# A two-block transformer kernel in fp32: the second feed-forward product accumulated over 16 k-tiles at a time instead of 8, and the adaLN loads of one gate moved ahead of the recurrence

## What is computed

```
mod = silu(c) @ w_ada + b_ada                 # 2048 x 12288, six groups g = 0..5
shift1, scale1, gate1, shift2, scale2, gate2 = split(mod, 6)
...                                           # block 1: pooling and stick-breaking attention
x = x + gate1 * (mixed @ w_o)                 # block 2: dilated attention and a gated recurrence
h2 = rms_norm(x, norm2_w) * (1 + scale2) + shift2
f = square(relu(h2 @ w_ff1)) @ w_ff2          # 2048 x 8192, then 8192 x 2048
x = x + gate2 * f
```

## Time and profile before

| | |
|---|---|
| median of three runs | 2578.6 us |
| the profiled execution | 2580.78 us |
| its span, first to last instruction | 2579.0 us |
| PE busy | 2512.8 us, 97% |
| DVE busy | 2021.8 us, 78% |
| ACT busy | 1276.7 us, 50% |
| mean granted TensorE clock | 0.998 |
| read from HBM | 659.4 MB, 256 GB/s over the span |

### The profile page before, as it was taken

One profiled execution on the slowest core, in us unless ns is written; L12 is line 12 of the kernel. 1 busy time (PEld: TensorE's weight loads), 2 busy tenths in 40 slices (PEclk: granted clock), 3 DMA queues, 4 the chain that ended last, 5 costly groups with the idle time before them and its releaser, 6 DMA issues.

```text
span 2579.0 us, 32612 instructions
## 1 busy us (share of the span) xinstructions
PE 2512.8 (97%) x12429; PEld 2110.6 (82%) x12429; DVE 2021.8 (78%) x2305; ACT 1276.7 (50%) x1657; POOL 265.5 (10%) x321
## 2 busy tenths in 40 slices
PE   6999999999999999999999999999999999999998
PEld 5878787877888888888887878887888888888887
DVE  6778979998988898989877798886865666665566
ACT  4544455334555445544445554556455544554453
POOL 1000120202020202020300001350000000020000
PEclk9999999999999999999999999999999999999999
DMA  9999869897989898989756766464566777766654
GB/s 347 332 346 328 300 194 354 321 337 243 325 292 350 286 367 279 355 292 357 267 169 224 234 198 185 141 225 164 189 215 227 231 225 230 233 213 189 194 189 147
DMA packets 298364, 663.66 MB, mean 257 GB/s; under 512 B 20752, under 2 KB 21104, under 8 KB 297184
## 3 DMA queue, kind: packets, MB, share of 16 engines
q1 hardware_dynamic: 294976, 650.21, 74.4%
q0 software_dynamic: 2656, 9.66, 1.1%
q10 hardware_dynamic: 576, 1.70, 0.2%
HBM read 659.39 MB, written 2.10 MB: 256 GB/s over the span
## 4 chain that ended last, share of the span: by engine, by line
PE 83%; DVE 8%; DMA 3%; issue 3%; ACT 3%; SPq 0%; DVEq 0%; POOL 0%; ACTq 0%
PE PS L645 82%; DVE WL L1520 3%; ACT WH L1107 2%; DVE ACC L1528 2%; DMA RAWX<-in_w_in 1%; DVE UQ L1520 1%; PE PS L648 1%; DMA RAW<-in_w_in 0%; DMA RAW<-in_w_ada 0%; DMA RAWX<-in_w_o 0%; DVE hn L1528 0%; DVE AL L1520 0%; DMA RAW<-in_w_ff 0%; DMA RAW<-in_w_a_up 0%; DMA RAW<-in_w_o 0%
## 5 line engine op out<-in xcount | busy, mean ns | idle before, releaser
L1107 ACT ACTIVATE WH<-RAW 128x1024 fp32r<-128x1024 f32 x569 | 602.5, 1059 | 770.2 <-PE PS L645 578.1
L1520 DVE TENSOR_TENSOR WL<-RAW,WH 128x1024 fp32r<-128x1024 f32 x569 | 710.9, 1251 | 341.3 <-ACT WH L1107 340.1
L645 PE MATMUL PS<-WH,AH 128*128 128x512 f32 x2052 | 811.5, 395 | 16.6 <-DVE WL L1520 9.8
L645 PE MATMUL PS<-WH,AL 128*128 128x512 f32 x2052 | 800.8, 390 | 0.0
L645 PE MATMUL PS<-WL,AH 128*128 128x512 f32 x2052 | 800.5, 390 | 0.0
L645 PE MATMUL PS<-HL,WH 128*128 128x512 f32 x2048 | 601.9, 395 | 6.3 <-DVE HL L1528 5.1
L645 PEld LDWEIGHTS PS<-WH,AH 128*128 128x128 f32 x2052 | 386.1, 188 | 103.4 <-DVE WL L1520 18.7
L645 PEld LDWEIGHTS PS<-WH,AL 128*128 128x128 f32 x2052 | 386.0, 188 | 81.9
L645 PEld LDWEIGHTS PS<-WL,AH 128*128 128x128 f32 x2052 | 386.3, 188 | 76.8 <-issue 0.2
L645 PEld LDWEIGHTS PS<-HL,WL 128*128 128x128 f32 x2048 | 349.4, 188 | 67.2
L645 PE MATMUL PS<-HL,WL 128*128 128x256 f32 x2048 | 364.0, 279 | 0.0
(11 more groups left out here) (251 smaller groups left out, 1966.2 us busy)
## 6 DMA issues: line engine op xcount, KB each, us to landing
RAW<-in_w_ff SPq DMA_DIRECT2D x337, 512.0 KB, 4.4
RAW<-in_w_ada SPq DMA_DIRECT2D x282, 512.0 KB, 5.1
RAW<-in_w_in SPq DMA_DIRECT2D x192, 512.0 KB, 4.5
RAWX<-in_w_ada SPq DMA_DIRECT2D x102, 512.0 KB, 5.6
RAWY<-in_w_ff SPq DMA_DIRECT2D x96, 512.0 KB, 4.1
RAWX<-in_w_ff SPq DMA_DIRECT2D x79, 512.0 KB, 5.5
RAWX<-in_w_in SPq DMA_DIRECT2D x48, 512.0 KB, 5.4
RAW<-in_w_out SPq DMA_DIRECT2D x32, 512.0 KB, 3.6
```

Of the source, the lines that this page charges most:

```text
L645: return e.matmul(o, l, r, start=start, stop=stop, skip_group_check=True)
L1107: return e.activation(o, i, f, **kw)
L1520: return e.tensor_tensor(o, a, b, op)
```

## The change

`ff2` now takes all 16 k-tiles of `AH`/`AL` at a time: four rounds of 32 `ff1` ticks and then four `ff2` blocks of 8 ticks, with no `ff1` block ahead. In `chunk_t` the second feed-forward part now also runs its pieces in pairs. In the load plan, the groups of the first feed-forward part are spread over weights 0 to 245 instead of 0 to 221 and are followed there by the first 16 items of group (1,2). The other 16 are spread over weights 6 to 29 of `in2` (ticks 454 to 477), where before 6 were spread over 4 to 27, 18 over 30 to 65 and 8 over 96 to 115.

```diff
     def ff(w1, w2):
         one = [w(w1, 0, 16, cb * 512) for cb in range(16)]
-        two = [[c for n in range(4) for c in w(w2, r * 8, 8, n * 512)] for r in range(8)]
-        out = one[0] + one[1]
-        for r in range(8):
-            if r < 7:
-                out += one[2 * r + 2] + one[2 * r + 3]
-            out += two[r]
-        return out
+        two = [[c for n in range(4) for c in w(w2, r * 16, 16, n * 512)] for r in range(4)]
+        return [c for r in range(4) for part in one[4 * r:4 * r + 4] + [two[r]] for c in part]
...
-    plan += spread(ff(I["w_ff1"][0], I["w_ff2"][0]), [ada1[5], ada2[0], ada2[1], ada2[3], ada2[4]], 0, 222, 10)
-    in2 = spread(in2, [ada2[2][24:]], 96, 116)
-    in2 = spread(in2, [ada2[2][6:24]], 30, 66)
-    plan += spread(in2, [ada2[2][:6]], 4, 28)
+    plan += spread(ff(I["w_ff1"][0], I["w_ff2"][0]), [ada1[5], ada2[0], ada2[1], ada2[3], ada2[4], ada2[2][:16]], 0, 246, 10)
+    plan += spread(in2, [ada2[2][16:]], 6, 30)
...
     def ff(name, at):
-        made = [(name + "1", cb, at + 8 * cb, 8) for cb in range(2)]
-        at += 16
-        for r in range(8):
-            if r < 7:
-                made += [(name + "1", 2 * r + 2 + c, at + 8 * c, 8) for c in range(2)]
-                at += 16
-            made += [(name + "2", 4 * r + n, at + 4 * n, 4) for n in range(4)]
-            at += 16
+        made = []
+        for r in range(4):
+            made += [(name + "1", 4 * r + c, at + 8 * c, 8) for c in range(4)]
+            made += [(name + "2", 4 * r + n, at + 32 + 8 * n, 8) for n in range(4)]
+            at += 64
         return made
...
-                b = 2 * (n % 4) if n < 28 else 2 * (n % 2)
+                b = 2 * (n % 4) if n < 12 else 2 * (n % 2)
...
-                    for run in ((0, 1), (2, 3)) if j < FG else ((0, 1, 2, 3),):
+                    for run in ((0, 1), (2, 3)):
...
-                    r = n // 4
-                    if n % 4 == 0 and c % 2 == 0:
-                        e.wait_ge(s_fl, (0 if name == "ff2" else 32) + 4 * r + 2 * (c // 2) + 2)
-                    if n == 31 and c == 3:
-                        chunk_end(j, q, c, AH, AL, 8 * (r % 2))
+                    if n % 4 == 0:
+                        e.wait_ge(s_fl, (0 if name == "ff2" else 32) + 2 * n + c + 1)
+                    if n == 15 and c == 7:
+                        chunk_end(j, q, c, AH, AL, 0)
                     else:
-                        chunk(j, q, c, c == 3, AH, AL, 8 * (r % 2))
+                        chunk(j, q, c, c == 7, AH, AL, 0)
...
-                k = 8 * (n // 2 % 2) + 4 * (n % 2) + 2 * t
+                k = 4 * (n % 4) + 2 * t
...
-                for name, at, step in (("wo", WO + 8, 8), ("ff2", IN2 - 12, 4), ("ob", OB + 4, 4)):
+                for name, at, step in (("wo", WO + 8, 8), ("ff2", IN2 - 24, 8), ("ob", OB + 4, 4)):
...
-                    if n < 28:
+                    if n < 12:
                         tt(acc, ps, acc, ALU.add).then_inc(s_ev["dve"], 1)
-                        if n >= 24:
-                            fp = (0 if name == "ff2" else 16) + 4 * (n - 24) + 2 * t
-                            if n == 24 and t == 0:
+                        if n >= 8:
+                            fp = (0 if name == "ff2" else 16) + 4 * (n - 8) + 2 * t
+                            if n == 8 and t == 0:
                                 e.wait_ge(s_g, gates[gate] + 4)
```

More of the change, by code:

```diff
@@ L365, in both @@
         name, n = self.all[q][:2]
-        return (name, n) in (("wo", 3), ("ff2", 31), ("oa", 0), ("ob", 3), ("fg2", 31)) or (name == "in2" and n >= 12)
+        return (name, n) in (("wo", 3), ("ff2", 15), ("oa", 0), ("ob", 3), ("fg2", 15)) or (name == "in2" and n >= 12)
     def ended(self, j):
@@ L862, in norm_gap @@
                 name = normed[at]
-                unused = bl.bank[bl.at[name, {"wo": 2, "ff2": 30, "ob": 2}[name]]] + 1
-                eng, count = evac_of[bl.at[name, {"wo": 2, "ff2": 30, "ob": 2}[name]]][1]
+                unused = bl.bank[bl.at[name, {"wo": 2, "ff2": 14, "ob": 2}[name]]] + 1
+                eng, count = evac_of[bl.at[name, {"wo": 2, "ff2": 14, "ob": 2}[name]]][1]
                 e.wait_ge(s_ev[eng], count)
@@ L1679, in evac @@
                     acc = mem["acc"][:, t, c]
-                    if n == 31 and t == 0:
+                    if n == 15 and t == 0:
                         e.wait_ge(s_half, 2 if name == "ff2" else 4)
@@ L1698, in evac @@
                     else:
-                        fp = (0 if name == "ff2" else 16) + 4 * (n - 28) + 2 * t
-                        if n > 28:
+                        fp = (0 if name == "ff2" else 16) + 4 * (n - 12) + 2 * t
+                        if n > 12:
                             if name == "ff2":
-                                e.wait_ge(s_ssq, 8 + 2 * (n - 28) + t - 1)
+                                e.wait_ge(s_ssq, 8 + 2 * (n - 12) + t - 1)
                             else:
-                                e.wait_ge(s_x1, x_count(tag, n - 29, t))
+                                e.wait_ge(s_x1, x_count(tag, n - 13, t))
                         e.wait_ge(s_fp, fp + 2)
-                        add_x(tag, n - 28, t, ps, mem["tmp"][:, t, :], ev)
+                        add_x(tag, n - 12, t, ps, mem["tmp"][:, t, :], ev)
                 elif name == "in2":
```

## The result

| | before | after |
|---|---|---|
| median on one chip | 2579.7 us (2577.1 to 2582.2) | 2593.4 us (2591.0 to 2597.3) |
| ratio | | 1.0052, 95% interval 1.004 to 1.0063 |
| span of the profiled execution | 2579.0 us | 2591.2 us |

The change makes the kernel slower by 0.5%. The predicted 2574.4 us was wrong in sign, and the measured time lies outside the range, above its end at 2583.5.

The account below looks back on a forecast made before the run. PE, busy for 97% of the span, was taken to bound the kernel. The terms summed to -4.2 us, taking the profiled 2580.8 to 2576.6, or 2574.4 as a median; the range was 2568 to 2583.5.

Parts of the forecast that it names:

- term 1: Both feed-forward parts: 64 fewer accumulation adds, 44 us of DVE work, give 0.
- term 2: `ff1` of the second feed-forward part: pairs space the matmuls closer, -2.6 us (bounds 2 to 3).
- term 3: Tick 423, at 1282 us: the old stall goes as gating moves away from group (1,4), -3.8 us.
- Term 7: Recurrence, four groups from 1446.73 us: freed of adaLN items, -5.5 us (bounds 3 to 6.6).
- Term 4: Gating of blocks n = 8 to 11, first part: DVE bursts beside adaLN items exceed the cover, +3.2 us (0 to 6).
- Term 5: Tick 434, six slots to four: weight 434 loads late in a bunch, +3.0 us (bounds 0 and 5.6).
- Term 6: Ticks 454 to 477: sixteen adaLN items on four slots put the load stream behind, +1.5 us (0 and 5.4).
- The rival that starved PE: Ticks 434 to 478: four slots starve PE at loads from about 5.1 us on, 2584.3 us; chance 0.15.
- The first rival: The lookahead swallows the new delays, terms 4 to 6 near 0, 2566.7 us; chance 0.22.
- The rival of falls of the clock: The clock falls at the new stalls of terms 4 and 5, +1.9 to +3.8 us, 2577; chance 0.15.

Follow-up runs that it names:

- experiment 3: The kernel before with all of the change's diff but the pairs and the load plan (rounds of 16 k-tiles alone): 2581.9 us, ratio 1.0004.
- experiment 9: The changed kernel with adaLN items placed as in the best plan so far and the raw ring kept aligned at tick 434: 2580.6 us, ratio 0.9999.
- experiment 4: The changed kernel with the ring's turn moved up to slot 0 at tick 434, so slots are in order: 2587.5 us, ratio 1.0028.
- experiment 7: The changed kernel with adaLN items of the first feed-forward part spread over weights 0 to 241 instead of 0 to 245: 2587.1 us, ratio 1.0025.
- experiment 1: The kernel before with one edit, the second feed-forward part running its pieces in pairs: 2577.4 us, ratio 0.9994.

## Why the prediction was wrong, step by step

**Terms 1, 2, 3 and 7 held.** The halved adds gave nothing by themselves, as said. The pairs gave 2.4 us for 2.6, the lost stall at tick 423 3.7 for 3.8. The freed recurrence gave 5.1 us from tick 479 to 497. Term 7 counted 5.5 in the four groups of the earlier trace rows, ticks 477 to 492, which are now

```profile
1465.55:1480.64 15.09, 15.09 (x74) 12.81 (x73) 8.76 (x14) 7.86 (x10) 0.00 (x0) 0.92 0.56 178
1480.64:1495.32 14.68, 14.58 (x76) 12.09 (x76) 12.02 (x22) 9.15 (x14) 0.00 (x0) 1.00 0.48 144
1495.32:1509.74 14.42, 14.42 (x79) 12.38 (x78) 11.60 (x24) 9.27 (x13) 0.00 (x0) 1.00 0.51 150
1509.74:1525.75 16.01, 14.87 (x78) 12.02 (x76) 14.70 (x26) 11.49 (x17) 0.00 (x0) 1.00 0.44 131
```

or 60.2 us for 63.9: 3.7 less, within the term's bounds of 3 to 6.6. The two groups with DVE busy for about 12 us take 14.7 and 14.4 us, near the 14.4 foretold; the one with 14.7 us of DVE takes 16.0, and the first still runs in part at the lower clock.

**Term 4, the gating: +7.9 for +3.2, above its bound of 6.** The step that failed is "a cover of 5.44 - 2.6 = 2.9 us". I took it from a place with no adaLN loads near and used it in a dense stretch, where around ticks 361 to 363 ACT's copies wait up to 3.1 us for loads of 6.6 us. There the work ahead of PE is only as far ahead as the loads let it be. The places were right (362, 363, 371, 379, 386, 387), and so were the sizes of two of the four blocks: 0.9 us for n = 9, as counted, and 0.7 for n = 10, counted as 0.6. Around these ACT's copies wait for PE, as term 4 assumed, all but one, which waits 2.4 us for a load at the end of n = 10:

```profile
1132.82 1.06 ACT L1096 ACTIVATE WH<-RAWX 128x1024 fp32r<-128x1024 f32 x1 [1.66 <-PE PS L635]
...
1160.92 1.06 ACT L1096 ACTIVATE WH<-RAW 128x1024 fp32r<-128x1024 f32 x1 [1.66 <-PE PS L635]
```

The other two, n = 8 and n = 11, came to 3.8 and 2.9 us where 0.6 and 1.1 were counted, and there the copies wait for loads. The size depends on where the gaps between groups fall: 3.1 us with the old plan (experiment 3), 7.9 with two others (the changed kernel, experiment 9). That the loads take the cover away is read from the traces; no run kept the gating and took the adaLN loads around it away.

**Term 5, the switch to four slots: +7.8 for +3.0, above its bound of 5.6.** The mechanism was the one described: an adaLN item and weight 434, two items back, then a bunch. Mis-sized were both its inputs. "Weight 434's load can start at 2.6 us after the start of tick 431" came to 4.4 (1312.20, with the tick's start at 1307.8), since the load before it had itself taken 6.26 us; and the bunch took 7.12 us where my end was 6.7. PE idled for 5.6 us instead of 2.5, and the clock fell behind it (0.97 over the stretch). Experiments 3, 4 and 7 show that neither the order of the slots nor the items alone is worth the loss. The 1.4 that the term subtracts for the kernel before wasn't the order alone either: with the same order and plan and lighter rounds, in experiment 3, it is gone. By the formula of the Trainium skill (DMA: Bandwidth & Descriptors, section on the anatomy of one DMA), which is fitted on GpSimd's path, each of these loads would take an estimated 3.2 us. The trace doesn't agree for loads in a bunch, 5.3 us in experiment 4 and 7.1 here.

**Term 6, in2: +2.5 for +1.5.** Within its bounds.

**What had no term: +6.7 at ticks 475 to 479.** I counted the lookahead of three ticks as cover for the weights, and it did cover the weights. I didn't ask what else stands in ACT's queue behind those early copies. The rival that starved PE (ticks 434 to 478, chance 0.15) came nearest, though not by its own account. It wanted loads of 5.1 us and more; over ticks 454 to 474 the medians are 4.6 us for a weight and 4.9 for an adaLN item, and the loads in the chain take 5.2 to 5.6. Its stream through `in2` was to cost 5.4 us and cost 2.5. Its price, 2584.3, was 9 us too low, because it lacked this stall and took the switch at 5.6 and term 4 at 3.2. The first rival, that the lookahead swallows it, is refuted at each of its three places.

**The clock.** The rival of falls of the clock came true beside the others, as a part of them. There are two, behind the stall of tick 434 and at tick 476, and the two stretches show 0.97 and 0.82. They are included above.

**The sum.** Terms 4, 5 and 6 were 10.5 us too low, the missing one 6.7, the good ones gave 0.7 less than counted (with term 7 at the 5.1 of ticks 479 to 497): -4.2 + 10.5 + 6.7 + 0.7 = +13.7, less 0.9 at the start of the kernel and 0.6 elsewhere, +12.2. Terms 4 and 5 and the missing one share one error: where copies wait for loads there is no slack to lend, and I took the slack from places where they didn't.

## What to carry to other kernels

Before placing extra work in a lookahead pipeline, see what the producer waits for at that very place: if its copies already wait for loads, count on no cover, however many ticks the code looks ahead. Count items per tick against slots and the load time of that stretch (in `in2`, before the recurrence, 1.45 a tick on four slots was free and 1.67 cost 1.8 to 2.5 us), and keep bursts, changes of ring and spread loads on different ticks. In an in-order queue, put small operands that the bottleneck needs soon ahead of big copies that may wait.

## What the runs showed beyond the question

The same stall doesn't always bring the clock down. In experiment 1, whose code is that of the kernel before up to its second feed-forward part, PE waited 1.77 us at tick 423 (before: 1.87), and the two ticks took 7.51 us at a clock of 1.00 where the earlier trace rows show 9.20 at 0.81:

```profile
1282.07:1289.58 7.51, 5.74 (x26) 4.43 (x24) 7.30 (x12) 2.12 (x2) 0.00 (x0) 1.00 0.44 137
```

1.7 us of term 3 are thus there in one of the two traces and not in the other. The Trainium skill (TensorE: Matmul & The Clock Gate, section on what is actually happening) says that the matmuls spent at the slow rate at a kernel's start differ between runs of one kernel; these two traces show a like difference behind a stall in the middle.

The first 192 ticks, alike in all twelve kernels, took between 595.7 and 603.7 us, more than any single term of this change. Differences of a few microseconds are to be read from the stretch that the edit touches, and the whole only from many runs.
